# Rows of an expert's tokens fetched by an indirect DMA and turned by transposes, and unread products on TensorE in waits of norms, router and mixers

## The reference

```
def moe_swiglu(x, router, wg, wu, wd):
    logits = (x @ router).astype(jnp.float32)
    top_v, top_i = lax.top_k(logits, TOP_K)          # 2 of 8 experts
    w = jax.nn.softmax(top_v, axis=-1)
    comb = jnp.einsum('blk,blke->ble', w, jax.nn.one_hot(top_i, N_EXPERTS))
    y = jnp.zeros_like(x)
    for e in range(N_EXPERTS):
        y = y + comb[..., e:e + 1] * swiglu(x, wg[e], wu[e], wd[e])
```

## Time and profile before

| | |
|---|---|
| median of 3 runs | 2593.2 us (2593.19 to 2593.28) |
| profiled execution, its own time | 2596.66 us |
| its span, first to last instruction | 2594.9 us |
| granted TensorE clock, mean | 0.944 of 2.4 GHz |
| busy: TensorE / VectorE / ScalarE / GpSimd | 2399.1 / 1639.1 / 1074.1 / 181.1 us |
| DMA | 456.43 MB, 176 GB/s mean |

### The profile page before, as it was taken

The page is one execution under the profiler, slowest core; times in us unless marked ns, Lnnn a source line. Parts: engine busy times, 40 slices in busy tenths (PEclk is TensorE's granted clock), DMA queues, the critical chain, the costliest instruction groups (busy, mean ns, idle before and its releaser), DMA issues.

```text
span 2594.9 us, 38245 instructions
## 1 busy us (share of the span) xinstructions
PE 2399.1 (92%) x14436; PEld 2069.6 (80%) x14436; DVE 1639.1 (63%) x2112; ACT 1074.1 (41%) x1450; POOL 181.1 (7%) x247
## 2 busy tenths in 40 slices
PE   8899898899999899899798997999999999999996
PEld 6788778876899888789687866787887878878786
DVE  4554853743665454457636633778787887878776
ACT  4332311321333334324122220566666666667662
POOL 0212111201000001202012010000000000000000
PEclk8999898998999989999898988899999999999998
DMA  5323311322444333234112320898898978889871
GB/s 197 105 87 134 131 66 41 111 82 98 152 163 163 127 130 106 95 134 142 54 50 83 110 73 32 325 327 289 300 329 297 335 284 303 319 296 332 291 278 64
DMA packets 122566, 456.43 MB, mean 176 GB/s; under 512 B 14056, under 2 KB 14474, under 8 KB 120018
## 3 DMA queue, kind: packets, MB, share of 16 engines
q1 hardware_dynamic: 118818, 432.66, 47.5%
q0 software_dynamic: 3632, 22.12, 2.4%
HBM read 443.72 MB, written 11.00 MB: 175 GB/s over the span
## 4 chain that ended last, share of the span: by engine, by line
PE 72%; DVE 17%; issue 6%; ACT 4%; POOL 1%; DVEq 0%; DMA 0%; SPq 0%; ACTq 0%; POOLq 0%
PE ps L726 7%; PE ps L728 7%; PE ps L727 7%; PE ps L773 6%; DVE weights_low L2255 4%; PE ps L1293 4%; PE ps L1295 4%; PE ps L1294 4%; PE ps L1315 3%; PE ps L1316 3%; PE ps L1317 3%; PE ps L1266 3%; PE ps L767 2%; DVE arena L1889 2%; PE ps L808 1%
## 5 line engine op out<-in xcount | busy, mean ns | idle before, releaser
L726 PE MATMUL ps<-u_high,tiles_high 128*128 128x288 f32 x1688 | 526.0, 312 | 17.5 <-DVE tiles_low L1718 17.5
L727 PE MATMUL ps<-u_low,tiles_high 128*128 128x288 f32 x1688 | 513.0, 304 | 0.0
L728 PE MATMUL ps<-u_high,tiles_low 128*128 128x288 f32 x1688 | 511.1, 303 | 0.0
L1718 DVE TENSOR_TENSOR tiles_low<-ring,tiles_high 128x1024 fp32r<-128x1024 f32 x238 | 298.1, 1255 | 201.6 <-ACT tiles_high L1374 200.2
L726 PEld LDWEIGHTS ps<-u_high,tiles_high 128*128 128x128 f32 x1688 | 332.1, 197 | 26.7 <-issue 24.6
L2255 DVE TENSOR_TENSOR weights_low<-expert_ring,weights_high 128x1024 fp32r<-128x1024 f32 x288 | 334.5, 1219 | 5.2 <-ACT weights_high L1627 2.0
L727 PEld LDWEIGHTS ps<-u_low,tiles_high 128*128 128x128 f32 x1688 | 332.6, 197 | 0.5
L728 PEld LDWEIGHTS ps<-u_high,tiles_low 128*128 128x128 f32 x1688 | 332.2, 197 | 0.0
L1374 ACT ACTIVATE tiles_high<-ring 128x1024 fp32r<-128x1024 f32 x238 | 250.6, 1054 | 170.9 <-DMA ring<-in_stream 81.0
L1293 PE MATMUL ps<-weights_high,u_high 128*128 128x512 f32 (+1 forms) x768 | 297.6, 388 | 22.9 <-DVE weights_low L2255 22.3
L2255 DVE TENSOR_TENSOR weights_low<-ring,weights_high 128x1024 fp32r<-128x1024 f32 x240 | 280.2, 1218 | 43.2 <-ACT weights_high L1627 42.1
(11 more groups left out here) (381 smaller groups left out, 3290.2 us busy)
## 6 DMA issues: line engine op xcount, KB each, us to landing
ring<-in_stream SPq DMA_DIRECT2D x530, 512.0 KB, 4.2
expert_ring<-in_stream SPq DMA_DIRECT2D x288, 512.0 KB, 5.6
arena<-in_state POOLq DMA_DIRECT2D x8, 1024.0 KB, 5.1
state_s<-arena POOLq DMA_DIRECT2D x8, 1024.0 KB, 4.3
const<-in_const SPq DMA_DIRECT2D x1, 2052.5 KB, 12.0
arena<-in_const POOLq DMA_DIRECT2D x2, 832.0 KB, 4.9
h<-in_x SPq DMA_DIRECT2D x1, 1152.0 KB, 5.0
y<-acc POOLq DMA_DIRECT2D x1, 1152.0 KB, 4.4
```

The source lines that it names most:

```text
L726: mm(out, hi[k], uh[:, k, :], start=k == 0, stop=False)
L727: mm(out, hi[k], ul[:, k, :], start=False, stop=False)
L728: last = mm(out, lo[k], uh[:, k, :], start=False, stop=k == KD - 1)
L1718: tt(t_low[:, q % HELD, :], ring[:, (t % RING) * TILE:(t % RING + 1) * TILE], t_high[:, q % HELD, :].bitcast(F32), ALU.subtract).then_inc( ...
```

## The change

There are two parts.

1. **The gather.** When `utok` has been written, POOL stores its 288 rows of 4 KB into a tensor in HBM (`token_rows`). VectorE writes each token's number into `token_no`; three products with one column of the one-hot matrix and these numbers (`place_list`) give the list of the tokens in the 128 places, which VectorE copies as integers (`place_token`). POOL issues an indirect DMA by this list: 128 rows of 4 KB from `token_rows` into `xrows`, which lies on the first block of `utok`. TensorE turns `xrows` into the two banks with 8 transposes in place of the 24 products. The list of the next expert is made in group 2 of the current one, and its rows are loaded once the transposes have read the old ones.
2. **Unread products.** `warm(n)` makes n products of ones with a block of h, 288 columns each, into a bank that nobody reads before it is written anew. They stand in `norm` (3 before and 5 behind the wait for `rt_ready`, in six of the seven norms), `prep` (2), the first level of `gla` (6), `gdn` (12), the last sums of `ssd` (4), and in the routing (2 + 2 + 4 + 2 + 6).

Semaphores are also regrouped (`router_in` becomes `expert_dma`, `utok_ps` goes into `logit_ps`). The core of the diff:

```diff
@@ norm
                 last.then_inc(sumsq_ps, 1)
+                if k < 3 * DEPTH:
+                    warm(3)
+                    pe.wait_ge(rt_ready, k + 1)
+                    warm(5)
+
+            def warm(n, at=M + 5):
+
+                for i in range(n):
+                    mm(bank(at)[:, 0:TOK], C("ones"), h[:, i % KD, :], start=True, stop=True)
@@ prep
                 last.then_inc(small_ps, 1)
+                warm(2)
                 pe.wait_ge(glr_ready, L + 1)
@@ out_sums
+                if n == SSD:
+                    warm(4, M + 3)
                 pe.wait_ge(osq_ready, m + 1)
@@ gla
                     if lv == 0:
+                        warm(6)
                         pe.wait_ge(cross_zero, L + 1)
@@ gdn
                 fill(L, GDN, 8)
+                warm(12)
                 pe.wait_ge(qk_ready, L + 1)
@@ experts, TensorE
+                    if b < 2:
+                        warm(2, 1)
...
-                pe.wait_ge(sel_ready, 1)
                 pe.wait_ge(expw_ready, 1)
+                warm(4, 1)
+                pe.wait_ge(sel_ready, 1)
...
+                def place_list(out):
+
+                    for b, (t0, nt) in enumerate(TB):
+                        last = mm(out, gath[0:nt, b, :], token_no[0:nt, b:b + 1], start=b == 0, stop=b == 2)
+                    last.then_inc(pos_ps, 1)
+
+                warm(2, 1)
                 pe.wait_ge(pos_ready, 1)
+                pe.wait_ge(gath_ready, 1)
+                place_list(bank(1)[:, 0:1])
+                warm(6, 0)
...
-                        pe.wait_ge(gath_ready, it * 2 + 1)
+                        pe.wait_ge(expert_dma, it * 16 + 64)
+                        pe.wait_ge(pos_ready, it + 2)
                         pe.wait_ge(expert_added, it * 3 + 3)
                         for k in range(KD):
-                            for b, (t0, nt) in enumerate(TB):
-                                last = mm(bank(k // 4)[:, PLACES * (k % 4):PLACES * (k % 4 + 1)], utok[0:nt, b, P * k:P * k + P],
-                                          gath[0:nt, b, :], start=b == 0, stop=b == 2)
+                            last = nc.tensor.transpose(bank(k // 4)[:, PLACES * (k % 4):PLACES * (k % 4 + 1)],
+                                                       xrows[:, P * k:P * k + P], C("ident"))
...
+                                if m == 0 and j == 2:
+                                    pe.wait_ge(expert_added, it * 3 + 5)
+                                    pe.wait_ge(gath_ready, it * 2 + 3)
+                                    place_list(bank(M + 4)[:, 0:1])
@@ experts, VectorE
+                for b in range(3):
+                    ts(token_no[:, b:b + 1], bank(M)[:, 32:33], float(P * b), None, ALU.add)
...
+                dve.wait_ge(pos_ps, 2)
+                cp(place_token, bank(1)[:, 0:1]).then_inc(pos_ready, 1)
...
+                            if j == 3:
+                                dve.wait_ge(pos_ps, it + 3)
+                                cp(place_token, bank(M + 4)[:, 0:1]).then_inc(pos_ready, 1)
@@ GpSimd, layer 1
+                    pool.dma_start(token_rows[0:2 * P].rearrange("(b p) c -> p b c", p=P), utok[:, 0:2, :]).then_inc(expert_dma, 16)
+                    pool.dma_start(token_rows[2 * P:TOK], utok[0:SAMP, 2, :]).then_inc(expert_dma, 16)
+                    pool.wait_ge(expert_dma, 48)
+                    def gather_rows():
+                        G.tensor_tensor(pool_turn, token_no[:, 0:1], token_no[:, 0:1], ALU.add).then_inc(turn_taken, 1)
+                        G.indirect_dma_start(xrows, None, token_rows, bass.IndirectOffsetOnAxis(ap=place_token, axis=0)
+                                             ).then_inc(expert_dma, 16)
+                    pool.wait_ge(pos_ready, 2)
+                    gather_rows()
...
+                            pool.wait_ge(gather_ps, it * 2 + 2)
+                            pool.wait_ge(turn_taken, it + 1)
+                            pool.wait_ge(pos_ready, it + 3)
+                            gather_rows()
```

More of the change, by code:

```diff
@@ L394, in build @@
         hid_ready = semaphore("hid_ready")
-        router_in = semaphore("router_in")
+        expert_dma = semaphore("expert_dma")
         logit_ps = semaphore("logit_ps")
-        utok_ps = semaphore("utok_ps")
+        turn_taken = semaphore("turn_taken")
         sel_ready = semaphore("sel_ready")
@@ L574, in build @@
         logit, sel, wts = [e_carve(3 * 8).rearrange("p (b e) -> p b e", b=3) for _ in range(3)]
+        token_no = e_carve(3)
+        place_token = e_carve(1).bitcast(I32)
+        pool_turn = e_carve(1)
         posm = e_carve(3 * 9).rearrange("p (b e) -> p b e", b=3)
@@ L584, in build @@
         utok = e_carve(3 * D_MODEL).rearrange("p (b c) -> p b c", b=3)
+        token_rows = nc.dram_tensor("token_rows", [TOK, D_MODEL], F32, kind="Internal").ap()
+        xrows = utok[:, 0, :]
         etanh, yt = acc_t[:, 0:1024].rearrange("p (a c) -> p a c", a=2), acc_t[:, 1024:2048]
@@ L1216, in experts @@
                                                    u[:, k, t0:t0 + nt], C("ident"))
-                last.then_inc(utok_ps, 1)
+                last.then_inc(logit_ps, 1)
+                pe.wait_ge(expw_ready, 1)
+                warm(4, 1)
                 pe.wait_ge(sel_ready, 1)
-                pe.wait_ge(expw_ready, 1)
                 d, before, on = bank(M), C("strict", 0, 128), C("ones")
@@ L1228, in experts @@
                     last = mm(d[0:nr, c:c + 8], (before if c == 16 else on)[0:32, 0:nr], sel[0:32, 2, :], start=False, stop=True)
-                last.then_inc(pos_ps, 1)
+                mm(d[:, 32:33], before, on[:, 0:1], start=True, stop=True).then_inc(pos_ps, 1)
+                def place_list(out):
[3 more added lines that the diff above has]
+                warm(2, 1)
                 pe.wait_ge(pos_ready, 1)
+                pe.wait_ge(gath_ready, 1)
+                place_list(bank(1)[:, 0:1])
+                warm(6, 0)
                 mm(bank(M)[0:32, 0:32], C("ident", 0, 32), C("ident", 0, 32), start=True, stop=True).then_inc(expert_step, E_STEPS)
```

16 lines of the change are left out of this document (12 added, 4 removed).

## The result

The changed kernel takes 2557.85 us (median of 4 runs, 2555.62 to 2563.83) where the kernel before takes 2593.24 (4 runs, 2593.19 to 2605.43). The ratio is 0.9846 with a 95% interval of 0.9816 to 0.9875: 32 to 48 us faster. The forecast was 2531, with 2513 to 2554 as its range and 2521 to 2542 for its own mechanism. The sign was right. The median lies 4 us above the wide range; the ratio stands for 40 us, or 2553, just inside its upper end, and that end was drawn to take in rivals. By either figure the narrower range was missed: the forecast gain of 62 us is 1.5 to 1.8 times the measured one.

What follows compares the result with a forecast made beforehand. TensorE was taken as the bound (72% of the chain, mean clock 0.944), VectorE next. Gather 41, routing 7 and other unread products 15 sum to 63 us off: 2531 us forecast, range 2513 to 2554, own range 2521 to 2542.

Steps and rivals of the forecast that it cites:

- The gather, experts 2 to 8: Start of the seven later experts: transposes replace one-hot products, net 5.9 us each, 41 us less in all, bounds 35 to 44.
- rival 5: Experts: VectorE absorbs half of the gather's gain by later low parts, 20 us less gain, 2551; chance 6%.
- The indirect load: POOL's load of the next expert's rows: 5 us, hidden under 57.2 us of cover, costing nothing.
- rival 3: Indirect load emits its 128 rows singly at 0.54 us each, 73 us against 57.2 of cover: about 2715; chance 4%.
- rival 2: Each expert's start: transposes let the clock fall, scatter at the low level, 2.1 us times 7: 2546; chance 7%.
- Routing and the first expert: From first router product to first gate product: 7 us less, bounds 9 less and 10 more.
- at 0.09 each they take 4.35: Routing: the 48 router passes take 4.35 us instead of 7.92; with 1.9 of unread products between, 1.6 less.
- At 1.2 GHz it would be 3.1 more: Routing: the other case for the router passes, at the low clock, costing 3.1 us more.
- The four products before the counting: Routing: four unread products ahead of the counting products, 1.9 us more, with 1.3 gained from the clock in those 18 passes.
- The other unread products: Filled waits in mixers, norms and projections hold the clock: 15 us less, bounds 0 (less 3 of overshoot) and 24.
- what ran at the low level behind it: Mixers, GLA, projections: each filled wait priced by the low-clock work following it, such as 3.4, 3.4 and 3.2 us.
- Rival 1: The clock doesn't follow the filling: the 15 us become -3 and routing 2, giving 2553; chance 14%.

Runs made afterwards that it cites:

- gather alone: The changed kernel with every unread product removed, leaving list, indirect load and transposes: 2547.59 us, ratio 0.9811 to the kernel before.
- gather alone, again: The same code without unread products, run once more on another chip: 2551.58 us (2547.10 to 2563.14, 6 runs).
- routing's products only: The changed kernel with only the unread products of the routing and of its norm kept: 2555.6 us.
- load without cover: The changed kernel without unread products, GpSimd holding each indirect load of experts 2 to 8 until the expert's last product is done: 2633.43 us.
- in the kernel before: The kernel before, one-hot gather kept, with the unread products added at the same places except the routing's last six: 2605.63 us, ratio 1.0018.
- mixers' and norms': The changed kernel without the unread products of the routing and its norm; those of mixers, small projections and other norms stay: 2554.44 us.
- norms' and sums' only: The changed kernel with only the unread products of the norms (not the routing's) and of the mixers' last sums: 2543.56 us, ratio 0.9803.
- small, GLA, delta only: The changed kernel with only the unread products of the small projections, the first GLA level and the delta mixer: 2558.51 us.

## Why the prediction was right or wrong

Two counts carry this section. Both are of single profiled executions, so the lines of equal code show how far one such figure can be trusted. The first is worked out from windows of 1 us ahead of 1590 us: a window with clock c has 2 x (1 - c) us at the low level, and TensorE's busy time in it is shared out in that proportion. The last column is the start of the first router product.

```
                          TensorE busy at 1.2 GHz   TensorE idle   first router product
same instructions ahead of the router's norm:
before                    201                       139            1597.66
gather alone              193                       141            1594.16
gather alone, again       217                       136            1599.38
routing's products only   216                       140            1602.59
load without cover        229                       135            1604.78
with unread products there:
changed                   219                        97            1607.00
in the kernel before      194                       102            1599.42
mixers' and norms'        200                       100            1601.53
norms' and sums' only     185                       122            1591.21
small, GLA, delta only    204                       121            1599.22
```

The second is by how many us VectorE's same instruction comes later (or earlier, with a minus) than in the kernel before, at ten points given by their time there.

```
                          92   148   224   596   959  1040  1149  1298  1451  1588
changed                  3.1   1.6   9.1   8.1   6.5   1.4   9.5   9.2  11.7   9.3
mixers' and norms'       3.2   2.7   2.8  -1.6  -3.2  -0.8   6.4   6.3   6.3   3.9
gather alone             0.0   0.0  -0.1  -0.2   0.7  -0.1  -0.1  -1.8  -3.4  -3.5
gather alone, again      3.1   5.1   5.3   2.1   2.1   2.1   2.1   0.4   1.2   1.7
routing's products only  1.2   0.9   8.4   8.3   8.4   8.4   8.4   6.6   5.0   4.9
load without cover       0.2   0.2   0.2  -1.9   0.1   0.1   7.3   7.2   7.2   7.1
```

**The gather, experts 2 to 8: right.** 41 us forecast, 44.1 measured, at the upper bound of 44, by the steps named: the gate starts 5.71 us after the transposes (5.95 forecast), and VectorE's tiles, low parts and addition end last. The 0.4 us more per expert are of the size of the list's 0.2, which seems to have cost nothing, and of the transposes, 1.03 instead of 1.3. VectorE at 91.75 of 105.80 did not absorb any of it (rival 5 out).

**The indirect load: right in its effect, the size low.** 6.9 us to landing against 5, issue 0.95 against 0.54 for a direct store. Rows are not emitted one at a time at that price (rival 3 out). The load without cover shows that hiding was the condition: 9.5 us each.

**The transposes and the clock: right.** The window 2069.96:2076.00 stands at 1.00 with eight transposes at its head (rival 2 out). The rule of the Trainium skill (TensorE: Matmul & The Clock Gate, Part 4: PE-mode transpose) would have the clock low there; eight transposes among other products don't bring that about.

**Routing and the first expert: wrong by 8 us.** 7 less forecast, 1.1 more measured, below the bound of 10 more. The step that failed is "at 0.09 each they take 4.35", a clock at the full level throughout the router's products: it fell within the first sixteen of their 48 passes, ahead of the first of the four unread products, and router and transposes took 15.6 us instead of the 9.9 of the sum. "At 1.2 GHz it would be 3.1 more" stood there as the other case, and I took the wrong one. The four products before the counting were priced at 1.9 and took 3.9, most of it at the low level. These two terms, 5.7 and 2.0, are the 8 us. The part of the gather was sized about right: from the first product behind the one-hot matrix to the gate 17.0 us (1635.47 to 1652.51), where 16 was forecast and 20.8 stood before, with a load of 8.1 us beside the stream. Without any unread product, the gather alone has its first addition into h 32.0 us after the copy of its first logits; the kernel before had 34.9 and the changed one 33.4.

**The other unread products: wrong, and the largest error.** 15 less forecast, 9.3 more in the profiled execution; between medians 6.9 more than the gather alone (2554.44 against 2547.59) and 2.9 more than its repeat. The step that failed is to add up "what ran at the low level behind it" over the filled waits, as if every other low stretch stayed as it was. The named stretches did go (those at 97, 586, 671, 903, 942, 1022 and 1511 in the kernel before have no counterpart), and the second table shows time coming back at filled places: 1.5 us from 92 to 148, where the GLA level stands, 5.1 from 959 to 1040 (small projections and GLA level of the second layer), 2.4 behind 1451. But 7.5 us were lost from 148 to 224 and 8.1 from 1040 to 1149, where nothing is filled, by new low stretches at 161, 175 and 195 and at 1086 and 1117. TensorE had no idle time in the 4 us ahead of these. In all the low level lasted 232 us ahead of 1590, as before.

Those two groups aren't shown to be the unread products' doing. The kernel with only the routing's has the first, at 161, 174 and 195, and the kernel without cover, which has no unread product at all, the second, at 1084, 1098 and 1118:

```profile
1085.00:1091.00 6.00, 6.00 (x27) 5.98 (x28) 0.00 (x0) 0.71 (x2) 0.00 (x0) 0.50 0.21 77
```

The second group stands in all three kernels with the full filling of mixers and norms, and in one of the eight other executions whose order of products is unchanged; whether the filling makes it likelier is open. With equal code the first router product began anywhere from 1594.16 to 1604.78, a spread of 10.6 us, so the 9.3 is an outcome of this execution as much as of the change. What is shown is that the 15 us didn't come: TensorE's busy time at the low level was 185 to 219 us with these products and 193 to 229 without, and the kernel before with them gained 4 us at most. What the filling surely took away is low time in which TensorE stood idle, which costs nothing: 31 us (232 - 201) before, 13 (232 - 219) in the changed kernel. At the delta mixer of the first layer 13.6 us were low before, with 6 us of work in them; after the filling 6.8 us were low, with the same 6. So nothing of the 1.2 us taken there came back. At the small projections of the first layer the clock fell ahead of the filling.

**The rivals.** Rival 1, the clock doesn't follow the filling, has the closest number, 2553, and in part by luck. By its own sign, stretches behind the filled waits still near 0.5, it came true at the delta mixer, the first small projections and within the router, and not at the seven stretches named above; its number fits because others came in their place. It priced the overshoot at 3 us and the routing at 2 less, where the profiled execution had 9.3 and 1.1 more, and gave the gather 41 instead of 44.1. It was given 14%, though rows in hand spoke for it: TensorE busy with one-hot products for 15 us at 0.50. That row was a warning and not a proof: of the 37 low stretches ahead of 1590 in the kernel before, 28 with 181 us in all had 0.9 us or more of idle time in the 4 us ahead of them, and 9 with 51 us had less than 0.5.

**What stays open.** Why the same instructions get a low stretch in one run and not in the next. A shift of the start by 2 us didn't bring it about, so "it hangs on the point in time" is not shown either; only that it isn't the instructions alone. The difference of 4 to 8 us between the gather alone and the norms' version is of the size of this spread, and so is what the unread products ahead of the router cost.

## What to carry to other kernels

Before a wait is filled to hold the clock, add up the work that ran at the low level behind it, not the time, and look whether the clock falls behind the wait or already ahead of it. Then measure the time from one fixed instruction to the end, not the stretch behind the wait: the stretches that were filled away here went, and others came where nothing had been changed. A gather by products can go to an indirect load whenever its list is known well ahead; the test is whether the issue stands further ahead of its reader than issue and landing, here 8 us, and the gain is then what the next engine in line leaves, not the products' time. Where runs of one program spread by 10 us, a part of a few us has to be tried apart and beside its base, several times, before it is kept.

## What the runs showed of the hardware

One program's profiled spans were 2545.4 and 2551.0 us on two chips with nothing changed, and its mean clock over the first 200 us 0.93 and 0.90; on one chip six runs of it took 2547.10 to 2563.14 us; single executions of this kernel can't be compared to a few us. An indirect load of 128 rows of 4 KB took GpSimd 0.95 us to issue (1.76 at the median without its cover) and 6.7 to 8.1 us to land. After a wait of 8.42 us the clock was low for the transposes and most of the scatter that followed; the Trainium skill (TensorE: Matmul & The Clock Gate, HAM oscillation — how this bites in real kernels) has the rule that a wait for a DMA lets the next tile start at the low clock; the trace agrees. The clock also falls with TensorE busy throughout: in the kernel with the routing's unread products alone it was 1.00 from 156 to 160 us with TensorE busy for 4.00 of 4, behind a row of 32 four-column passes it was 0.50 from 161 to 167 with 6.00 busy of 6, and the same instructions ran at 1.00 in the gather alone. And it can fall after a short wait although the work ahead of it was dense: in the changed kernel's routing it was 1.00 with 4.00 us busy of 4 up to 1604.60, then came 2.35 us of waiting, and it was 0.50 from 1609 on with TensorE busy.
